# Hybrid decoder step on one core: convolution moved into the input projection and between head steps, fewer constant products on TensorE

## The reference, cut to what matters

```python
z = hn @ w_in                                   # 2080 columns
c_q, c_kv, k_r, qb, kb, vb, ga, gb = split(z)   # 256,128,32,384,384,384,256,256
g = ga * sigmoid(gb)
...
y = depthwise_conv(g_ext, conv_w) + conv_b      # 31 taps, 256 channels, causal
conv = silu(layernorm(y, ln_g, ln_b))
...
x = x + concat([mla, dilated, conv]) @ w_out    # 384 + 384 + 256 rows
```

## Time and profile before

| | us |
|---|---|
| median of 3 runs | 2124.94 |
| lowest, highest | 2123.55, 2128.51 |
| profiled execution, own time | 2134.3 |
| its span | 2132.5 |
| TensorE busy | 2105.2 (99% of the span) |
| VectorE, ScalarE busy | 1570.0, 1281.0 |
| mean granted TensorE clock | 0.993 |

### The profile page before, as it was taken

The page is one execution under the profiler, slowest core; times in us unless marked ns, Lnnn a source line. Parts: engine busy times, 40 slices in busy tenths (PEclk is TensorE's granted clock), DMA queues, the critical chain, the costliest instruction groups (busy, mean ns, idle before and its releaser), DMA issues.

```text
span 2132.5 us, 40828 instructions
## 1 busy us (share of the span) xinstructions
PE 2105.2 (99%) x15616; PEld 1816.5 (85%) x15616; DVE 1570.0 (74%) x3530; ACT 1281.0 (60%) x2519; POOL 111.2 (5%) x138
## 2 busy tenths in 40 slices
PE   8999999999999999999999999999999999999998
PEld 7766699999999888788886656999999998887886
DVE  6675489977899876676675744899678997766766
ACT  5454345558888665565563543455588886655654
POOL 2100010000000010100021000100000001001000
PEclk9999999999999999999999999999999999999999
DMA  9443327776666888898664433377766668988786
GB/s 318 148 154 119 139 80 253 246 260 222 217 217 218 271 311 289 300 316 277 226 227 159 143 120 139 115 260 247 252 220 216 216 215 289 313 287 296 257 269 216
DMA packets 141841, 481.77 MB, mean 226 GB/s; under 512 B 26034, under 2 KB 48594, under 8 KB 135232
## 3 DMA queue, kind: packets, MB, share of 16 engines
q1 hardware_dynamic: 129248, 438.45, 60.1%
q0 software_dynamic: 10496, 40.42, 5.3%
q10 hardware_dynamic: 1904, 0.29, 0.1%
HBM read 475.82 MB, written 104.21 MB: 272 GB/s over the span
## 4 chain that ended last, share of the span: by engine, by line
PE 97%; DVE 2%; issue 0%; DMA 0%; ACT 0%; DVEq 0%
PE ps L1166 34%; PE ps L1213 33%; PE ps L857 4%; PE ps L817 3%; PE ps L901 3%; PE ps L1178 3%; PE ps L1129 2%; PE ps L909 2%; PE ps L1137 1%; PE ps L1133 1%; PE ps L847 1%; PE ps L866 1%; PE ps L1013 1%; PE ps L997 1%; PE ps L1152 1%; PE ps L1000 1%
## 5 line engine op out<-in xcount | busy, mean ns | idle before, releaser
L2116 DVE TENSOR_TENSOR parts<-region,parts 128x1024 fp32r<-128x1024 f32 x512 | 625.8, 1223 | 302.4 <-ACT parts L1457 300.0
L1166 PE MATMUL ps<-tokens_hi,parts 128*128 128x256 f32 x4096 | 760.5, 284 | 0.0
L1457 ACT CAST parts<-region 128x1024 fp32r<-128x1024 f32 x512 | 538.6, 1052 | 271.7 <-PE ps L1213 214.1
L1213 PE MATMUL ps<-parts,parts_hw 128*128 128x512 f32 x3072 | 699.6, 389 | 0.0
L1213 PEld LDWEIGHTS ps<-parts,parts_hw 128*128 128x128 f32 x3072 | 575.8, 188 | 125.8 <-DVE parts_hw L2166 6.9
L1166 PEld LDWEIGHTS ps<-tokens_hi,parts 128*128 128x128 f32 x4096 | 636.6, 188 | 1.0 <-issue 0.5
L1166 PE MATMUL ps<-parts_hw,parts 128*128 128x256 f32 x2048 | 573.8, 280 | 0.0
L1166 PEld LDWEIGHTS ps<-parts_hw,parts 128*128 128x128 f32 x2048 | 386.5, 189 | 0.0
L1503 ACT ACTIVATE big<-ps 128x256 f32<-128x256 f32 (+31 forms) x252 | 131.6, 522 | 147.0 <-PE ps L1166 146.9
L1491 ACT CAST parts_hw<-big 128x256 fp32r<-128x256 f32 x256 | 170.5, 666 | 0.7 <-DVE big L2177 0.7
L1484 ACT ACTIVATE region<-region 128x128 f16<-128x128 f16 x512 | 169.2, 436 | 0.0
(11 more groups left out here) (324 smaller groups left out, 2251.8 us busy)
## 6 DMA issues: line engine op xcount, KB each, us to landing
region<-in_peer_uT SPq DMA_DIRECT2D x256, 512.0 KB, 4.1
region<-in_peer_v SPq DMA_DIRECT2D x256, 512.0 KB, 4.7
out<-in_state_win_k SPq DMA_DIRECT2D x112, 384.0 KB, 4.8
out<-in_state_win_v SPq DMA_DIRECT2D x112, 384.0 KB, 4.9
big<-in_state_win_k SPq DMA_DIRECT2D x48, 192.0 KB
big<-in_state_win_v SPq DMA_DIRECT2D x48, 192.0 KB, 3.8
region<-in_w_out SPq DMA_DIRECT2D x4, 2048.0 KB, 8.7
big<-in_peer_wq SPq DMA_DIRECT2D x4, 2048.0 KB, 14.1
```

What stands on the lines that cost most here:

```text
L1166: mm = pe.matmul(ps[:, j % ZB, 0:SEQ], a, hp[b][:, c, :], start=(c == 0 and n == 0), stop=(c == KD - 1 and n == 2))
L1213: mm = pe.matmul(ps[:, 2 * half + t, :], w_t[a][:, 128 * t:128 * t + 128], v_t[b][:, 512 * half:512 * half + 512], start=(j == 0 and n == ...
L1457: act.copy(hi_t[n % HIGHS], rows_t[n % ROWS]).then_inc(high[l], 1)
L2116: dve.tensor_tensor(lo_t[n % ROWS], rows_t[n % ROWS], hi_t[n % HIGHS], ALU.subtract).then_inc(low[l], 1)
```

## The change

The gates' columns become chunk 1 of the projection, and the gated columns are turned into `gT` right after chunk 2. VectorE rotates queries and keys in two calls with 36 instructions instead of 18, applies 3 taps after the queries and 24 after the keys, and 5 in each of steps 0 to 6. Step 7 has the samples' convolution, step 8 the turned `yt`, step 9 the statistics, step 10 the square root, step 11 the normalization; the tail keeps `ycT` alone. The constant products ahead of `PT` stay for heads 9 to 11, those ahead of `yt` and `ycT` go, and three new ones stand ahead of `ext`. Buffers of the convolution move to places that are free for longer. The diff, cut:

```diff
-ZCH = [(0, 416), (416, 384), (800, 384), (1184, 384), (1568, 512)]
+ZCH = [(0, 416), (1568, 512), (416, 384), (800, 384), (1184, 384)]
+TAPS_AHEAD = (3, 24)
+TAPS = (5, 5, 5, 5, 5, 5, 5)
+CONV_STEP = (7, 8, 9, 10, 11)
...
         jobs += [(("z", c, t), "A") for t in range(2)]
+        if c == 2:
+            jobs += [(("gT", 0), "V"), (("gT", 1), "V")]
...
-    jobs += [(("gT", 0), "V"), (("gT", 1), "V")]
...
+        if s == CONV_STEP[1]:
+            jobs += [(("yt", t), "A") for t in range(3)]
...
-    jobs += [(("yt", t), "A") for t in range(3)]
...
+                    if c == 2:
+                        pe.wait_ge(g_ready, 1)
+                        for i in range(2):
+                            turn("gT", i, parts=tokens(z, GA + 128 * i))
...
-                    if u >= 5:
+                    if u >= 9:
                         keep_busy(("PT", u), 2)
...
+                keep_busy(("ext",), 3)
                 pe.wait_ge(spread_set, 1)
...
+                    if s == CONV_STEP[1]:
+                        pe.wait_ge(y_ready, 1)
+                        for t, (t0, m) in enumerate(TOK):
+                            turn("yt", t, parts=[...])
...
-                keep_busy(("yt", 0), 2)
-                pe.wait_ge(y_ready, 1)
-                for t, (t0, m) in enumerate(TOK):
-                    turn("yt", t, parts=[...])
-                keep_busy(("ycT", 0), 3)
                 pe.wait_ge(ln_ready, 3)
...
-                        if c == 4 and g >= 2:
+                        if c == 1 and g >= 2:
                             e = act.activation(dst, o[32 * g:32 * g + NB, cols], ACT.Sigmoid)
...
+                    if s == CONV_STEP[3]:
+                        roots(5, slice(9, 12))
...
                 input_low(2)
+                wait_moved(dve, "z", 1, 1)
+                dve.tensor_tensor(z[:, :, GA:GA + CC], ..., z[:, :, GB:GB + CC], ALU.mult).then_inc(g_ready, 1)
...
                 wait_moved(dve, "z", 2, 1)
+                rotate_heads(QB)
+                some_taps(TAPS_AHEAD[0])
+                input_low(4)
+                wait_moved(dve, "z", 3, 1)
+                rotate_heads(KB)
                 dve.nop().then_inc(qk_ready, 1)
+                some_taps(TAPS_AHEAD[1])
...
-                    for n in range(5):
+                    some_taps(TAPS[s] if s < len(TAPS) else 0)
...
+                    if s == CONV_STEP[0]:
+                        samples_conv()
+                    if s == CONV_STEP[2]:
+                        conv_stats()
+                    if s == CONV_STEP[4]:
+                        conv_norm()
                 o = read("os")
...
+                conv_out()
```

More of the change, by code:

```diff
@@ L1085, in _ @@
                         mm.then_inc(product[now[0]], 1)
+                    if s == CONV_STEP[1]:
+                        pe.wait_ge(y_ready, 1)
+                        for t, (t0, m) in enumerate(TOK):
+                            turn("yt", t, parts=[(yT[:, c, t0:t0 + m], 128, m, 128 * c) for c in range(2)])
                 wait_moved(pe, "O", 2 * NH - 1)
@@ L1418, in _ @@
                             act.activation(dst, o[:, 0:384], ACT.Copy, scale=rdw[:, n:n + 1]).then_inc(moved_a[now[0]], 1)
+                    if s == CONV_STEP[1]:
+                        for t, (t0, m) in enumerate(TOK):
+                            o = read("yt", t)
+                            act.copy(yt[0:m, t, :], o[0:m, 0:CC]).then_inc(moved_a[now[0]], 1)
+                    if s == CONV_STEP[3]:
+                        roots(5, slice(9, 12))
                 for g in range(2 * HP):
@@ L1421, in _ @@
                     act.copy(mixT[:, g, 0:SEQ], o[:, 0:SEQ]).then_inc(moved_a[now[0]], 1)
[L1422 to L1425, removed]
                 for c in range(2):
@@ L1707, in _, with tap @@
-                settle()
+                dve.wait_ge(conv_ld, 32)
+                step(dve.memset(gT[:, :, 0:CW - 1], 0.0))
+                for c in range(2):
+                    o = read("gT", c)
+                    step(dve.tensor_copy(gT[:, c, CW - 1:CW - 1 + SEQ], o[:, 0:SEQ]))
+                    dve.tensor_copy(gsT[:, c, :, CW - 1], o[:, SEQ:T]).then_inc(moved_v[now[0]], 1)
+                wait_moved(dve, "gT", 1)
+                settle()
+                def tap(n):
+                    j, c = n // 2, n % 2
+                    y, x, w = yT[:, c, 0:SEQ], gT[:, c, j:j + SEQ], cwT[:, c, j:j + 1]
+                    if j == 0:
+                        last_tap[c] = step(dve.tensor_scalar(y, x, w, g_cb[:, c:c + 1], ALU.mult, ALU.add))
+                    else:
+                        dve.wait_ge(vstep[now[0]], last_tap[c])
+                        last_tap[c] = step(dve.scalar_tensor_tensor(y, x, w, y, ALU.mult, ALU.add))
@@ new lines, in rotate_heads @@
+                def rotate_heads(c0):
+                    for t in range(3):
+                        x = z[:, t, c0:c0 + 384].rearrange("p (h s c) -> p h s c", h=NH, s=2)
+                        tt = [r[:, 192 * t:192 * t + 192].rearrange("p (h c) -> p h c", h=NH) for r in (ra, rb)]
+                        step(rotate(x[:, :, 0, :], x[:, :, 1, :], cosB[:, t, :].unsqueeze(1).to_broadcast([P, NH, 32]),
+                                    sinB[:, t, :].unsqueeze(1).to_broadcast([P, NH, 32]), tt[0], tt[1]))
+                    settle()
@@ L1708, in _, with some_taps @@
+                taps = iter(range(2 * CW))
+                def some_taps(n):
+                    for _ in range(n):
+                        k = next(taps, None)
+                        if k is not None:
+                            tap(k)
+                wait_moved(dve, "z", 2, 1)
+                rotate_heads(QB)
[3 more added lines that the diff above has]
+                rotate_heads(KB)
                 dve.nop().then_inc(qk_ready, 1)
-                wait_moved(dve, "z", 4, 1)
@@ L1737, in _ @@
                 dve.tensor_copy(qlS[:, :, 0:NH], qlT[:, :, SEQ:T].rearrange("p h b -> p b h")).then_inc(spread_set, 1)
[L1738 to L1755, removed]
                 def past_max(b):
@@ L1904, in _ @@
[L1904 to L1907, removed]
-                    step(dve.tensor_reduce(yT[:, c, SEQ:T], t1, AX, ALU.add))
-                    settle()
-                    step(dve.tensor_scalar(yT[:, c, SEQ:T], yT[:, c, SEQ:T], g_cb[:, c:c + 1], None, ALU.add))
@@ L1921, in _ @@
-                dve.nop().then_inc(sq_ready[l], 1)
-                dve.wait_ge(std_ready[l], 5)
-                step(dve.reciprocal(stat[:, 9:12], stat[:, 9:12]))
-                settle()
-                for t, (t0, m) in enumerate(TOK):
-                    dve.tensor_scalar(yt[0:m, t, :], yt[0:m, t, :], bnst[0:m, t, 6:7], stat[0:m, 9 + t:10 + t],
-                                      ALU.subtract, ALU.mult).then_inc(ln_ready, 1)
-                for c in range(2):
-                    o = read("ycT", c)
-                    dve.wait_ge(sig_ready, c + 1)
-                    step(dve.tensor_scalar(ycs[:, 2, :], o[:, 0:T], g_lg[:, c:c + 1], g_lb[:, c:c + 1], ALU.mult, ALU.add))
-                    settle()
-                    dve.tensor_tensor(mixT[:, 6 + c, :], ycs[:, 2, :], ycs[:, c, :], ALU.mult).then_inc(moved_v[now[0]], 1)
-                    wait_moved(dve, "ycT", c)
+                conv_out()
```

93 lines of the change are left out of this document (50 added, 43 removed).

## The result

| | before | after |
|---|---|---|
| median of 6 runs each, us | 2124.85 | 2115.57 |
| lowest to highest | 2123.46 to 2128.51 | 2110.66 to 2118.32 |
| mean granted clock of the runs | 0.993 (profiled), 0.993 to 0.996 in its later executions | 0.991 to 0.995 |

The ratio is 0.995, interval 0.994 to 0.9959. The change made the kernel faster by 9.3 us where 21.4 were forecast. The time lies 12 us above the forecast of 2103.5 and above the range, which ended at 2113.

A forecast was written before the change was run, and what follows sets the result against it. TensorE, busy 2105.2 of 2132.5 us, was taken as the bound. Layer 0 at −10.1, layer 1 at −11.3 and clock 0 gave −21.4 us, so 2124.9 became 2103.5 us, with a range of 2096 to 2113.

The forecast's parts named there:

- Products ahead of heads 5 to 8: Head loop, steps 6 to 9: removing these constant products saves 7.33 us per layer, all on the chain.
- Tail: From `os` to `xo`: only the turned `ycT` stays, saving net 6.38 us in layer 0 and 7.55 in layer 1.
- VectorE ahead of `q`: VectorE's idle time there, 15.4 us, takes 14.0 us of added taps and rotation instructions; it just fits.
- slower: Rival: VectorE reaches 27 taps only when `q` is ready, TensorE stands 11.1 us per layer; 2129 us, chance 0.03.
- Products ahead of `ext`: Ahead of `ext`: six added instructions cost 2.58 us per layer and answer to the half clock at 1149.3.
- `gT` at zero: Its 1.06 us leaves the place ahead of `ext` and comes back behind chunk 2, without a wait: zero.
- New waits at 1.0 per layer: Head loop, steps 7 and 8: TensorE waits 1.0 us for the samples' convolution, between nothing and 2.46.
- Clock at zero: Both layers: two early half-clock stretches gone (−3.3), one new (+1.7), layer 1's long stretch reaching into `xo` (+1.6); together zero.
- a clock of at least 0.993: Sign expected in the changed profile: the granted clock should be at least 0.993.
- From the profiled execution to the median: Cut stretches are TensorE-bound in either, so 21.4 us comes off the median too, 9.4 us below the profiled execution.
- waits take the products' place: Rival, steps 6 to 9: VectorE and ScalarE set the length; half back gives 2111, all 2118; chance 0.16.
- the clock falls more often: Rival: three more stretches of half clock per layer at 1.67 us give 2113.5; chance 0.07.

The follow-up runs named there:

- products_only: The kernel before without the constant products ahead of heads 5 to 8; 2112.34 us, ratio 0.9941.
- conv_only: The changed kernel with the constant products ahead of heads 5 to 8 kept and without the three ahead of `ext`; 2118.36 us, ratio 0.9967.
- after_again: The changed kernel, unchanged, run again for a second trace; 2116.34 us, ratio 0.9949.
- before_again: The kernel before, unchanged, run again for a second trace; 2126.58 us, ratio 1.0005.
- tail_bare: The kernel before without the five constant products of the tail, ahead of `yt` and `ycT`; 2128.57 us, ratio 1.0013.
- after: The first profiled execution of the changed kernel, its fastest; 2110.66 us at a clock of 0.995.
- best1_bare: The changed kernel with samples' convolution in step 6, window's new-sample scores behind head 5's scaling, no constant products ahead of `ext` or in the head loop; 2095.03 us.
- products_back: The changed kernel with the two constant products ahead of each of heads 5 to 8 put back; 2121.55 us, ratio 0.9978.

## Why the prediction was wrong

*Products ahead of heads 5 to 8: 7.33 per layer, right as a size.* `products_only` brought 13.5 of 14.7 us. That in step 6 both move together held. That the wait for L1879 "stays" was nearly so: it was 0.8 to 0.9, and grew to 1.0 to 1.5 in the changed kernel.

*Tail: right.* 16.0 us against 15.7. The rows of `ycT` beside `xo` left no wait. In the pair compared the match has some luck in it: both tails ran partly at half clock, about 1.2 us per layer before and 0.9 after, and these nearly cancel.

*VectorE ahead of `q`: right.* From `q` to `qlT` TensorE took 14.09 us per layer before and 14.09 to 14.10 after, so the 27 taps fitted, and the rival "slower" had no ground.

*Products ahead of `ext`: right as a size* (2.45 against 2.58 per layer). That they answer to the half clock at 1149 fits the traces, as above, but it brings less than they cost, and in the kernel's second trace there was only one early stretch to save.

*`gT` at zero: the step that failed first.* The move costs its 1.06 in the projection (57.83 to 58.84 and 56.71 to 57.76 us), but taking it away ahead of `ext` gave nothing back: without the constant products a wait of 0.91 for VectorE's L1776 fills the place, with them 0.61 us of "issue" and a slightly longer run of products. I had moved the step in TensorE's stream and not asked what would end last ahead of `ext`. About 1.8 us in both layers.

*New waits at 1.0 per layer: undersized, and for the wrong place.* Their real sum was 3.1 in layer 0 and 2.9 in layer 1, less 0.9 of before: 2.0 to 2.2. I had named the samples' convolution, 2.46 at the upper end, and took the turned past as its cover. But `yt` was not what waited for it. The turned probabilities of the past, ahead of `yt`, needed the bank of head 8's scores, which stood behind the convolution on VectorE's queue. The constant products removed in the same change had been the cover there: `conv_only`, which keeps them, has no such wait.

*Clock at zero: the largest error.* In the table the rest of the loop's 4.4 (2.2), the 3.6 of `olT` and `mT` and `xo`'s 3.0 come to 8.8 us, and nearly all of it is half clock: `after_again` has 3.4, 7.5 and 6.0 us more of it in these stages than `before_again`, which at 1.67 us lost per 3.40 is 1.7, 3.7 and 3.0. Three things were missed. First, the credit of 3.3 for two early stretches came from a trace that had three of them, where the kernel's other trace had one; the stretches did go, but only one was there to lose. Second, the new waits brought a stretch of their own into step 8. Third, the stretch at the loop's end, which both kernels have, had been hidden for about a half by the tail's constant products under VectorE's chain, and lies on `mT`, `ycT` and `xo` in full once they are gone. I had allowed 1.6 for it in one layer. My own sign, a clock of at least 0.993, failed in 7 of the 11 executions of the changed kernel, and the 23.8 us near half clock became 27.3 in `after_again`. The mean clock over executions says the same more roughly: 0.993 to 0.996 before, mostly 0.991 to 0.993 after, and over the executions of one kernel 0.001 goes with about 2 us (before_again: 2124.4 at 0.995, 2126.6 at 0.994; changed kernel: 2110.7 at 0.995, 2117 to 2118 at 0.991).

*From the profiled execution to the median.* Subtracting the same 21.4 was safe for the work cut, not for the clock terms, as above. The tail, which that sentence counts among the TensorE-bound stretches, was set by VectorE's chain (`tail_bare`); its size held all the same, since the chain left the tail with the products. Against the trace of 2134.3 the changed kernel's 2110.7 would even have looked like a gain of 23.6 and confirmed the forecast.

Of the rivals, "waits take the products' place" and "the clock falls more often" were both true in part, each put at about 2111 to 2113.5; parts of both together give the result. I had taken them as alternatives, though a wait of TensorE is one of the things behind which the clock fell.

The Trainium skill's page "TensorE: Matmul & The Clock Gate", section "HAM oscillation — how this bites in real kernels", ties the fall to idle time of TensorE. The stretches in step 8 lie behind such idle time, in layer 0 waits of 1.33 and 1.76 us, as that section would have it, though the waits in its own case are longer. The one in the window from 200 to 212 us, with TensorE busy 12.00 of 12.00 us, does not fit it.

What stays open: why one and the same kernel has 3.4 us of half clock at the loop's end in one execution (`after`) and 10.2 in another (`after_again`), and whether the wait alone brings the stretch in step 8. It went with the wait in the traces; no run put an equal wait elsewhere. What the products ahead of `ext` do to the clock rests on the pattern over the traces alone, since no kernel was traced often enough with and without them.

## What to carry to other kernels

When filler work and real work are taken out of one stretch together, price them together: look at each edge of the remaining stream for what the filler was hiding, a late engine or a slow clock, since each part alone can look free. A step moved away from in front of a wait gives nothing until the thing waited for is early as well. And read a second trace of the kernel before one prices terms of the clock: here two executions of it differed by 10 us.

## What the runs showed of the hardware

Constant products on TensorE's own path bought little clock and cost more than they bought. Without any in the head loop the mean clock was 0.993 to 0.994 (`best1_bare`), with them ahead of seven heads and of `ext` 0.993 to 0.998 (`products_back`). Taking them away brought 13.5 us for heads 5 to 8 (`products_only`) and 10.4 for heads 9 to 11. What they could buy is less: the best clock seen, 0.998, was worth 6 us against that kernel's median.

In the tail, where TensorE waited for VectorE anyway, they paid. Without them the clock fell from 0.993 to 0.996 down to 0.990 to 0.992, and the kernel was 2.8 us slower (`tail_bare`).

The clock fell to half with TensorE busy throughout (200 to 210 us in `after_again`) as well as behind waits of 1.3 and 1.8 us. A stretch at half clock cost up to 1.67 us where it fell on work that TensorE's path needed, and less where VectorE's chain set the length: the tail took 9.54 us at a clock of 0.78 against 8.37.

Small products can meet gaps of "issue": 64 instructions on 96 columns took 1.51 us in one execution and, with gaps of 0.18 to 0.39 us between a few at a time, 3.95 us in another, from the same code.
